# A twelve-stage float32 network on one core: the first transfers, turns and roundings in another order

## The reference

```
h = rms_norm(x, norm_mix_pre[0])
h = neighbourhood_attention(h, na_w_qkv[0], na_w_o[0], na_rpb[0])   # 16 heads of 64, 4 rows of 64 tokens
x = x + rms_norm(h, norm_mix_post[0])
h = rms_norm(x, norm_ffn_pre[0])
x = x + rms_norm(swiglu(h, ...), norm_ffn_post[0])
```

## Time and profile before

| | |
|---|---|
| time, median of three runs | 1755.81 us |
| time of the profiled execution | 1756.92 us |
| its span | 1755.1 us |
| PE busy | 1746.5 us (100%) |
| PEld busy | 1497.9 us (85%) |
| DVE busy | 1226.0 us (70%) |
| ACT busy | 987.2 us (56%) |
| POOL busy | 109.4 us (6%) |
| read from HBM | 312.03 MB, 178 GB/s over the span |

### The profile page before, as it was taken

One profiled execution on the slowest core, in us unless ns is written; L12 is line 12 of the kernel. 1 busy time (PEld: TensorE's weight loads), 2 busy tenths in 40 slices (PEclk: granted clock), 3 DMA queues, 4 the chain that ended last, 5 costly groups with the idle time before them and its releaser, 6 DMA issues.

```text
span 1755.1 us, 25539 instructions
## 1 busy us (share of the span) xinstructions
PE 1746.5 (100%) x10100; PEld 1497.9 (85%) x10100; DVE 1226.0 (70%) x1897; ACT 987.2 (56%) x1580; POOL 109.4 (6%) x191
## 2 busy tenths in 40 slices
PE   8999999999999999999999999999999999999999
PEld 7888888888888888888888888888888888888887
DVE  5877765667776777467755787775587648878763
ACT  6666554545555655365545666654565446656551
POOL 1000000701110000000001010000000001100000
PEclk9999999999999999999999999999999999999999
DMA  8435554544343455544553334555354534335552
GB/s 331 183 145 196 191 225 168 225 175 159 140 154 131 165 195 201 217 148 189 192 216 139 127 146 175 209 192 214 129 212 189 216 129 169 138 145 216 192 215 73
DMA packets 45353, 314.74 MB, mean 179 GB/s; under 512 B 5024, under 2 KB 5536, under 8 KB 8240
## 3 DMA queue, kind: packets, MB, share of 16 engines
q1 hardware_dynamic: 44912, 312.54, 47.4%
q10 hardware_dynamic: 288, 0.52, 0.1%
q0 software_dynamic: 32, 0.03, 0.0%
HBM read 312.03 MB, written 1.05 MB: 178 GB/s over the span
## 4 chain that ended last, share of the span: by engine, by line
PE 99%; DMA 0%; DVE 0%; ACT 0%; ACTq 0%; issue 0%
PE P L419 96%; PE P L426 1%; PE P L718 1%; DMA ntm<-x_in 0%; ACT xx L1260 0%; PE P L1138 0%; PE P L620 0%; DVE xx L1811 0%; PE P L1058 0%; PE P L434 0%; PE P L1004 0%; DVE xs L1831 0%; PE P L752 0%; PE P L1081 0%; PE P L952 0%; ACTq L1749 0%
## 5 line engine op out<-in xcount | busy, mean ns | idle before, releaser
L1776 DVE TENSOR_TENSOR wl<-raw,wh 128x2048 fp32r<-128x2048 f32 x287 | 656.5, 2293 | 188.2 <-ACT wh L1232 169.0
L1232 ACT ACTIVATE wh<-raw 128x2048 fp32r<-128x2048 f32 x291 | 551.8, 1900 | 190.4 <-PE P L419 169.2
L419 PE MATMUL P<-xx,wh 128*128 128x512 f32 (+2 forms) x2800 | 652.1, 385 | 0.0
L419 PEld LDWEIGHTS P<-xx,wh 128*128 128x128 f32 (+1 forms) x2800 | 503.1, 188 | 98.0 <-issue 1.7
L419 PEld LDWEIGHTS P<-xx,wl 128*128 128x128 f32 x2688 | 344.3, 191 | 12.4
L419 PE MATMUL P<-xx,wl 128*128 128x256 f32 x2688 | 350.6, 283 | 0.0
L1361 ACT ACTIVATE ft<-P 128x256 f32<-128x256 f32 x240 | 90.3, 382 | 231.6 <-PE P L419 231.6
L419 PE MATMUL P<-wh,fhh 128*128 128x512 f32 x528 | 206.2, 390 | 0.0
L419 PE MATMUL P<-wh,fhl 128*128 128x512 f32 x528 | 205.5, 389 | 0.0
L419 PE MATMUL P<-wl,fhh 128*128 128x512 f32 x528 | 205.5, 389 | 0.0
L1939 DVE TENSOR_TENSOR fg<-P,ft 128x256 f32<-128x256 f32 x240 | 101.7, 424 | 121.2 <-ACT ft L1361 115.8
(11 more groups left out here) (326 smaller groups left out, 1466.2 us busy)
## 6 DMA issues: line engine op xcount, KB each, us to landing
raw<-w_all SPq DMA_DIRECT2D x289, 1024.0 KB, 4.8
nB<-rpb SPq DMA_DIRECT2D x4, 512.0 KB, 7.2
raw<-w_all SPq DMA_DIRECT2D x2, 512.0 KB, 6.6
xs<-x_in SPq DMA_DIRECT2D x1, 1024.0 KB, 7.7
fgb<-post SPq DMA_DIRECT2D x2, 512.0 KB, 6.3
out<-xs SPq DMA_DIRECT2D x4, 256.0 KB, 2.0
C<-cst SPq DMA_DIRECT2D x1, 769.0 KB, 8.4
ntm<-x_in ACTq DMA_DIRECT2D x2, 256.0 KB, 4.8
```

What stands on the lines that cost most here:

```text
L419: return t_.on.matmul(o, l, r, start=start, stop=stop, skip_group_check=True)
L1232: a.on.activation(o, i, ACT.Copy).then_inc(*hi.up((m,)))
L1776: v.on.tensor_tensor(o, i, h.bitcast(F32), ALU.subtract).then_inc(*lo.up(m))
```

## The change

The order of the first transfers, of the first turns and of the first roundings is another one; nothing else of the program differs.

- The eight gain columns of the first norm come with the identity (tile `C`, now 136 columns in the first transfer); the wait for the parameters (`s_prm`) moves from the head of ACT's, DVE's and POOL's lists to behind the start.
- ACT's queue fetches features 0 to 511 of both token tiles. SP's queue fetches: identity and gains; columns 0 to 511 of piece 0; columns 512 to 1023; the second row of piece 0; piece 1; features 512 to 1023 of both token tiles; the parameters; piece 2.
- The first quarter of x is turned in two parts of two blocks (the second into bank 1), with three warm transposes behind instead of five. `turn(0, 0, 1)` and `turn(0, 1, 1)` move in PE's list to behind the 16 products `high(1, i, t)` of piece 1, and in ACT's and DVE's lists to behind `ahead(0)`, that is behind piece 1 and ahead of piece 2.
- DVE rounds the first 512 columns of piece 0; ACT's `first_high(0)` does the other 512.

```diff
-            q.on.dma_start(C[:, 0:128], cst[:, 0:128]).then_inc(*s_ident.up(0))
+            q.on.dma_start(C[:, 0:136], cst[:, 0:136]).then_inc(*s_ident.up(0))
+            for h in range(2):
+                q.on.dma_start(raw[0][:, halfs(h)], w_all[0, :, halfs(h)]).then_inc(*s_first[h].up(0))
+            q.on.dma_start(raw[0][:, 1024:], w_all[0, :, 1024:]).then_inc(*s_raw[0].up(0))
+            fetch(1)
+            for t in range(2):
+                q.on.dma_start(nx[:, t, halfs(1)], placed(t, halfs(1))).then_inc(*s_x[t][1].up(0))
             q.on.dma_start(PR[:, :], prm).then_inc(*s_prm.up(0))
-            q.on.dma_start(raw[0][:, 0:1024], w_all[0, :, 0:1024]).then_inc(*s_first.up(0))
-            q.on.dma_start(nx[:, 1, :], placed(1, slice(0, D))).then_inc(*s_x[1][0].up(0))
-            q.on.dma_start(raw[0][:, 1024:], w_all[0, :, 1024:]).then_inc(*s_raw[0].up(0))
-            for m in range(1, RAW):
-                fetch(m)
+            fetch(2)
...
 PE, values_start
                 high(0, 1, 1)
-                turn(0, 1, 1)
                 low(0, 1, 0)
                 low(0, 1, 1)
                 for part in (high, low):
                     for i in range(2):
                         for t in range(2):
                             part(1, i, t)
+                    if part is high:
+                        for t in range(2):
+                            turn(0, t, 1)
 PE, na
                 warm(2, 7)
-                turn(0, 0, 0)
-                turn(0, 0, 1)
-                warm(2, 5)
+                turn(0, 0, 0, (0, 1))
+                turn(0, 0, 0, (2, 3), 1)
+                warm(2, 3)
                 values_start(banks)
 ACT
             def first_high(i):
-                a.wait_ge(*(s_raw[0] if i else s_first).of(0))
-                for hf in range(2):
+                a.wait_ge(*(s_raw[0] if i else s_first[1]).of(0))
+                for hf in range(1 - i, 2):
...
             def na():
-                turn(0, 0, 0)
+                turn(0, 0, 0, (0, 1))
                 first_high(0)
-                turn(0, 0, 1)
+                turn(0, 0, 0, (2, 3), 1)
                 turn(0, 1, 0)
                 first_high(1)
                 ahead(0)
+                turn(0, 0, 1)
                 turn(0, 1, 1)
                 ahead(1)
                 all_squares(0)
                 ahead(5)
+                a.wait_ge(*s_prm.of(0))
...
             for h in range(2):
-                a.on.dma_start(nx[:, 0, halfs(h)], placed(0, halfs(h))).then_inc(*s_x[0][h].up(0))
+                a.on.dma_start(nx[:, h, halfs(0)], placed(h, halfs(0))).then_inc(*s_x[h][0].up(0))
 DVE
             def na():
-                turn(0, 0, 0)
+                v.wait_ge(*s_first[0].of(0))
+                v.on.tensor_copy(wh[0][:, halfs(0)], raw[0][:, halfs(0)]).then_inc(*lo.up("first"))
+                turn(0, 0, 0, (0, 1))
                 first_low(0)
-                turn(0, 0, 1)
+                turn(0, 0, 0, (2, 3), 1)
                 turn(0, 1, 0)
                 first_low(1)
                 ahead(0)
+                turn(0, 0, 1)
                 turn(0, 1, 1)
                 ahead(5)
+                v.wait_ge(*s_prm.of(0))
```

More of the change, by code:

```diff
@@ L110 @@
 _at = 0
-for _name, _n in [("ident", 128), ("tri", 512), ("fox", 384), ("ssd", 128), ("gla", 128), ("seg", 256), ("blk", 128),
+for _name, _n in [("ident", 128), ("gain", 8), ("tri", 512), ("fox", 384), ("ssd", 128), ("gla", 128), ("seg", 256), ("blk", 128),
                   ("eps", 1), ("one", 1)]:
@@ L249, in build @@
         s_raw = [signal(f"s_raw{i}", 16) for i in range(RAW)]
-        s_first = signal("s_first", 16)
-        s_x = [[signal(f"s_x0{h}", 16) for h in range(2)], [signal("s_x1", 16)]]
+        s_first = [signal(f"s_first{h}", 16) for h in range(2)]
+        s_x = [[signal(f"s_x{t}{h}", 16) for h in range(2)] for t in range(2)]
         s_ident, s_prm, s_cst, s_gu, s_dist = (signal(n, 16) for n in ("s_ident", "s_prm", "s_cst", "s_gu", "s_dist"))
@@ L294, in build, with gain @@
         assert len(PL) == BASE[10]
+        def gain(s, c):
+            name, l = GAINS[s]
+            return par(name, l, c) if s else C[:, CCOLS["gain"] + c:CCOLS["gain"] + c + 1]
         def width(m):
@@ L419, in mul, with turn @@
                 return t_.on.matmul(o, l, r, start=start, stop=stop, skip_group_check=True)
-            def turn(s, t, q):
-                b = xbank(s, t, q)
+            def turn(s, t, q, js=(0, 1, 2, 3), b=None):
+                b = xbank(s, t, q) if b is None else b
                 claim(b)
-                t_.wait_ge(*(s_x[t][q * (1 - t)].of(0) if s == 0 else vx.of("x", s - 1, q, t)))
-                for j in range(4):
+                t_.wait_ge(*(s_x[t][q].of(0) if s == 0 else vx.of("x", s - 1, q, t)))
+                for j in js:
                     k = t_.on.transpose(P[b][:, toks(j)], (xs if s else nx)[:, t, (4 * q + j) * 128:(4 * q + j + 1) * 128], ident)
-                k.then_inc(*tx.up(("turn", s, t, q)))
-                held[b] = [(vx, "lo", s, t, 4 * q + 3)]
+                k.then_inc(*tx.up(("turn", s, t, q, js)))
+                held[b] = [(vx, "lo", s, t, 4 * q + js[-1])]
             def factors(s, b=6):
@@ L1252, in enter, with turn @@
                         a.wait_ge(*ax.of("sq", s, h, t))
-            def turn(s, t, q):
-                b = xbank(s, t, q)
-                name, l = GAINS[s]
-                a.wait_ge(*tx.of("turn", s, t, q))
-                for j in range(4):
+            def turn(s, t, q, js=(0, 1, 2, 3), b=None):
+                b = xbank(s, t, q) if b is None else b
+                a.wait_ge(*tx.of("turn", s, t, q, js))
+                for j in js:
                     c = 4 * q + j
                     a.on.activation(xh[:, c, toks(t)], P[b][:, toks(j)], ACT.Identity, bias=0.0,
-                                    scale=par(name, l, c)).then_inc(*ax.up(("hi", s, t, c)))
+                                    scale=gain(s, c)).then_inc(*ax.up(("hi", s, t, c)))
             def squares(s, h, t):
-                a.wait_ge(*(s_x[t][h * (1 - t)].of(0) if s == 0 else vx.of("x", s - 1, h, t)))
+                a.wait_ge(*(s_x[t][h].of(0) if s == 0 else vx.of("x", s - 1, h, t)))
                 a.on.activation(SQJ[s][:, t, halfs(h)], (xs if s else nx)[:, t, halfs(h)], ACT.Square, bias=0.0, scale=1.0,
@@ L1803, in enter, with turn @@
                 v.wait_ge(*ax.of("sq", s, 1, 1))
-            def turn(s, t, q):
-                b = xbank(s, t, q)
-                name, l = GAINS[s]
-                v.wait_ge(*ax.of("hi", s, t, 4 * q + 3))
-                for j in range(4):
+            def turn(s, t, q, js=(0, 1, 2, 3), b=None):
+                b = xbank(s, t, q) if b is None else b
+                v.wait_ge(*ax.of("hi", s, t, 4 * q + js[-1]))
+                for j in js:
                     c = 4 * q + j
-                    v.on.scalar_tensor_tensor(xl[:, c, toks(t)], P[b][:, toks(j)], par(name, l, c),
+                    v.on.scalar_tensor_tensor(xl[:, c, toks(t)], P[b][:, toks(j)], gain(s, c),
                                               xh[:, c, toks(t)].bitcast(F32), ALU.mult,
@@ L2459, in dve_program @@
             v.wait_ge(*s_ident.of(0))
-            v.wait_ge(*s_prm.of(0))
             na()
@@ L2719, in laid_out @@
     cst, dist = constants()
+    cst[:, CCOLS["gain"]:CCOLS["gain"] + 8] = inputs["norm_mix_pre"][0].reshape(8, 128).T
     arrays = dict(w_all=w_all, x_in=inputs["x"], w_gu=inputs["gla_w_gate_up_2"], cst=cst, dist=dist, prm=prm,
```

11 lines of the change are left out of this document (5 added, 6 removed).

## The result

| | before | changed |
|---|---|---|
| time, median of five runs each | 1755.81 us (1754.95 to 1757.62) | 1763.45 us (1762.36 to 1764.43) |
| ratio | | 1.0044, 95% interval 1.0033 to 1.0054 |
| profiled execution, its span | 1756.92, 1755.1 us | 1764.43, 1762.6 us |

The changed kernel is 7.6 us slower where 2.8 was forecast. The time lies outside the stated range, on the side of the rivals B and D, which both came true.

A forecast was written before the change was run, and what follows sets the result against it. PE, busy 1746.5 of 1755.1 us, was taken as the bound. 1.7 won at the front, 0.5 given back for a turn in the stream and 4.0 of new waiting gave 2.8 lost: 1758.6 us, range 1756.8 to 1761.4.

The forecast's parts named there:

- B: Rival, PE's new wait at piece 2: the clock falls there, costing 1.5 to 2; total +4.5, 1760.3 us; chance 0.28.
- D: Rival, first transfers: the front gains nothing, the product forecast at 11.98 stays at 13.66; +4.5, 1760.3 us; chance 0.15.
- Where it turns over: Piece 2: ACT's moved turns delay its rounding, so PE waits 4.0 us more; its second product comes 2.8 us later.
- What lies behind: After piece 2: ACT's squares and root 3.9 later, `high(3)` 3.47 behind `high(2)`; nothing counted, at worst 0.3.
- just in time: Piece 3: `low(3)` is ready at 31.7 and PE needs it at 31.8, so no wait was counted.
- Transfers to the first products: First row of piece 0: second half lands at 7.2, bounds 6.8 and 7.6, so the second product starts at 7.87.
- the clock holds: Products behind piece 2's waits: the sum kept them at the high clock level, 0.2275 us apart, with no slow-clock term.
- double failure: Both the clock falling at piece 2 and no gain at the front: +6.2, left out of the range.
- 1.7 won at the front: Start up to the second tile's low part: the product behind it begins at 11.98 in place of 13.66, 1.68 us won.

The follow-up runs named there:

- Moved turns alone: The kernel before with only the two turns moved, in the lists of PE, ACT and DVE: 1762.99 us, ratio 1.0041.
- turns early: The changed kernel with both moved turns back in PE's list ahead of `low(0, 1, 0)`, ACT's and DVE's lists as changed: 1757.83 us, ratio 1.0012.
- late turns: The changed kernel with ACT and DVE taking the two moved turns behind piece 2 instead of ahead of it: 1759.56 us, ratio 1.0024.
- dense source: The kernel turns early with piece 0 laid in HBM so that each transfer of it reads one block without gaps: 1755.84 us, ratio 1.0001.
- changed with the dense source: The changed kernel with piece 0 laid in HBM so that its transfers read blocks without gaps: 1761.32 us, ratio 1.0035.
- warm fill: The changed kernel with 34 transposes into a free bank ahead of piece 2 in PE's list: 1761.52 us, ratio 1.0034.
- split row: The kernel before with piece 0's first row in two 256 KB transfers, ACT waiting for each half and rounding both: 1755.08 us, ratio 1.0001.
- start order: The kernel before with one warm transpose for five and the second tile's first turn behind two products instead of four: 1755.78 us, ratio 1.0000.
- before with a dense source: The kernel before with piece 0 laid in HBM without gaps for its transfers: 1755.19 us, ratio 0.9998.
- whole row: The kernel turns early with piece 0's first row in one 512 KB transfer, DVE still rounding half: 1755.52 us, ratio 0.9999.
- x by tile: The kernel before with the first row in two transfers and x's quarters on the changed kernel's queues: 1758.74 us, one run.
- parameters first: The kernel turns early with the parameters fetched right behind the identity, as before: 1757.63 us, ratio 1.0012.

## Why the prediction was wrong

**The main step held.** *Where it turns over* put 4.0 us of new waiting on ACT's `wh` and DVE's `wl`, 0.5 for the turn in the stream, ACT idle until PE's transposes, and the rounding of piece 2 behind them at once. Measured: 4.05, 0.45, idle 5.65, and 21.83 + 2.02 = 23.85. One reading in it was wrong without a cost: piece 2 was not in SBUF from 14.4 on but landed at 16.8, 5 us before ACT came to the moved turns. Moved turns alone shows it with nothing else changed, turns early removes it. *What lies behind* was in order too: 29.28 is 3.47 behind 25.81, as in the earlier trace rows, and `low(3)` opened no wait. That it was "just in time" is what late turns ran into.

**The first failed step is "Transfers to the first products": "I take a landing at 7.2, bounds 6.8 and 7.6."** It landed at 8.9, outside the bounds, and the 1.7 us to be won came out as -0.1. Nor did x's second quarter take 5.9 us to land, but 7.0. The step took bytes ahead in the queue, at the rate of a single 1 MB transfer, as the only thing that sets a landing. It held the DMA engines' delivery to be the same whatever the shape and order of the transfers. From 4 to 6 us they delivered 146 GB/s where before they delivered 331; from a dense source the landing is 7.1 (changed) and 7.3 (turns early). Rival D had this outcome, with a doubt about what is beside a transfer, and a chance of 0.15. The rows gave a warning of how wide the bounds should be: two equal transfers of 256 KB took 3.7 and 5.9 us, 2.2 us apart, and the bounds were 0.4 us to either side.

**The second is that the clock holds.** The sum has no term for the clock behind the mark. Rival B's reason against a fall, that a product breaks the wait, did not count: it fell in all four profiles that have both waits open (the changed kernel twice, moved turns alone, changed with the dense source) and not with the wait filled. Its price, 1.5 to 2, was low for the first profile (2.96), fair for the second (1.5), and the medians of warm fill and the changed kernel give 2.0 to 2.6. One wait by itself did not do it: late turns has 1.83 us at the high level and keeps it. The rule of the Trainium skill, TensorE: Matmul & The Clock Gate, section "Why this matters for your kernels", which the prediction set beside B, agrees with the trace in what it warns of: the clock fell, here behind waits of 1.80 and 1.82 us.

Then 2.8 + 1.8 (front: DVE's turn at 13.37, where 11.57 was forecast) + 2.96 = 7.6. The double failure, B with D, was named with +6.2 and left out of the range. The range treated the two as if they would not come together; each had something in the profile for it.

**One more flaw, in the yardstick.** The profiled execution of before took 1.1 us more than the median, and the prediction carried that difference over. It lay, as far as the profiles show, at the very place that was being changed: in those of before, split row, start order and before with a dense source the span less the mark is 1731.5 to 1731.8, while the mark goes from 21.2 to 23.6. The spans of before in 114 executions beside these kernels ran from 1752.7 to 1755.2, with medians of 1753.2 to 1754.1 by group; less 1731.5 that makes, as an estimate, marks of 21.2 to 23.7, and 21.7 to 22.6 for the medians. The 23.56 of the earlier trace rows is the late end. So part of "1.7 won at the front" was there in most executions already, and against the medians the changed kernel's front is not 0.12 but, by the same estimate, 1.0 to 1.9 later, which is the size of what turns early keeps (+1.91). It would also be why start order, whole row, split row and before with a dense source, all with marks of 21.2 to 22.0, show no gain; that is argued from these numbers and not tested by a run. What decides from run to run is open; the profiles differ in when the identity lands (2.6 to 3.3) and in when the clock rises (5.8 to 14.9).

**Left open.** The strided halves deliver little when the strided second row and piece 1 stand right behind them (141 to 170 GB/s from 4 to 6 us, 202 with the parameters ahead), and 287 and 327 GB/s when x's quarters or its whole second tile do. So what stands behind them seems to count, but no run has the halves alone, or the second row alone, from a dense source, and the mechanism wasn't separated further. Split by partitions (4 KB lines) the row was late too, with the slow stretch from 6 to 8 us, so the length of a line is not the whole of it.

## What to carry to other kernels

When an instruction is moved later in the list of its producer, look up what stands behind its consumer in the next engine's list: here two turns of 1 us each held back the rounding of a piece that had landed at 16.8 until 23.85, and the work behind that piece is the next wait. An opened wait on a busy TensorE costs its length, and it can cost products at half the clock behind it (two waits of 1.8 us did here, one of 1.83 didn't), so price both, and give the joint case its chance when two rivals have the same sign. Where the change touches the stretch that differs from run to run, compare with the spans of all runs before using one profile as the base.

## What the runs showed of the hardware

- Two transfers of 256 KB that read 2 KB of every 8 KB, followed by 512 KB that read 4 KB of every 8 KB, moved 146 to 161 GB/s from 4 to 6 us with x's beside them (turns early and the changed kernel twice); the same bytes with all three from a source without gaps 259 and 292 (turns early and changed with the dense source).
- With x's rows behind them in place of the strided row, two such transfers moved 327 GB/s (split row, whole rows) and 287 GB/s (x by tile, quarters).
- Two waits of TensorE with one product between them lost the high clock, in the second wait: 1.80 and 1.82 us (changed), 2.03 and 1.11 us (parameters first, risen at 5.77 and fallen at 9.18). One wait alone did not: 1.83 us (late turns), 1.31 us (start order). 34 transposes of 128 x 128 in the place of the first two kept it up too (warm fill).
- DVE rounds 512 float32 columns in 0.43 us; ACT takes 0.63.
